# Recurrence turns: the first token-shift of the next feature tile ahead of the cumulative scan, the next weights' bf16 split in mid-turn

## The reference, cut to what matters

```
z_rw = z_rw + mu_shift * (z_prev - z_rw)
r, k, v, zw, za, zg = split(z_rw)
w_log = -softplus(-(rw_w0 + tanh(zw) @ rw_w2)) - 0.5 ; decay = exp(-exp(w_log))
state = state * w + (state @ a) b^T + v k^T          # for each token
y = state @ r  -> group norm, + bonus, * gate
```

## Time and profile before

| | |
|---|---|
| time, median of 3 | 1773.59 us (1773.27 to 1776.62) |
| profiled execution | 1781.12 us |
| its span, first to last instruction | 1779.3 us |
| mean granted TensorE clock | 0.985 of full speed |
| PE busy | 1659.7 us, 93% |
| DVE, ACT, POOL busy | 756.4 us (43%), 562.1 us (32%), 452.4 us (25%) |
| the recurrence's turns | about 155 to 484 us of the span |

### The profile page before, as it was taken

How to read it: one execution, slowest core, us unless ns; L and a number is a source line. 1 busy time by engine, 2 the same in 40 slices (tenths; PEclk the granted TensorE clock), 3 DMA queues, 4 the chain that set the end, 5 groups by cost and what they waited for, 6 DMA issues and landing times. The chain is left out here.

```text
span 1779.3 us, 35511 instructions
## 1 busy us (share of the span) xinstructions
PE 1659.7 (93%) x15497; PEld 864.6 (49%) x15690; DVE 756.4 (43%) x1040; ACT 562.1 (32%) x882; POOL 452.4 (25%) x236
## 2 busy tenths in 40 slices
PE   4999888898899999799999899999999999999997
PEld 2454655566644555444444344444444444444443
DVE  5596545555433555411311288332314233232328
ACT  5323444444323555321212156330202121121200
POOL 1221311222201112022522213461505232332220
PEclk9999999999999999999999999999999999999999
DMA  9851001000111200221210211331212020212002
GB/s 356 259 190 31 15 4 30 12 9 22 47 29 48 60 1 1 104 74 35 62 44 24 95 48 36 95 95 48 64 42 83 19 76 24 71 35 83 1 0 95
DMA packets 105775, 109.72 MB, mean 62 GB/s; under 512 B 2592, under 2 KB 82610, under 8 KB 105394
## 3 DMA queue, kind: packets, MB, share of 16 engines
q1 hardware_dynamic: 105648, 107.82, 18.7%
HBM read 101.52 MB, written 4.19 MB: 59 GB/s over the span
## 5 line engine op out<-in xcount | busy, mean ns | idle before, releaser
L218 PE MATMUL tokens_ps<-a_hi,z 128*128 128x512 bf16 x941 | 246.0, 381 | 4.0 <-ACT ff_r L2426 3.0
L674 PE MATMUL ff_ps<-ff_hi,c_lo 128*128 128x512 bf16 x503 | 190.6, 379 | 0.6
L674 PE MATMUL ff_ps<-ff_hi,c_hi 128*128 128x512 bf16 x501 | 189.9, 379 | 1.4 <-DVE z L2530 0.9
L674 PE MATMUL ff_ps<-ff_lo,c_hi 128*128 128x512 bf16 x501 | 189.9, 379 | 0.6
L2530 DVE TENSOR_TENSOR z<-ff_ps,z 128x512 f32<-128x512 f32 x128 | 88.3, 690 | 205.1 <-PE ff_ps L674 204.4
L2426 ACT ACTIVATE ff_r<-tokens_ps,cols 128x1024 f32<-128x1024 f32 x32 | 35.6, 1113 | 436.2 <-PE tokens_ps L218 427.0
L2353 POOL TENSOR_TENSOR z<-z 128x1024 bf16<-128x1024 f32 x28 | 62.2, 2220 | 351.6 <-ACT z L2349 351.6
L218 PEld LDWEIGHTS tokens_ps<-a_hi,z 128*128 128x128 bf16 x960 | 94.1, 98 | 116.6 <-issue 4.0
L218 PE MATMUL tokens_ps<-a_lo,z 128*128 128x512 bf16 x469 | 140.9, 380 | 0.6
L2518 DVE TENSOR_TENSOR ff_r<-ff_r 128x1024 f32<-128x1024 f32 x32 | 41.1, 1285 | 226.2 <-ACT ff_r L2426 226.2
L195 POOL TENSOR_TENSOR mg_wlo<-mg_stage,mg_whi 128x1024 bf16<-128x1024 f32 x21 | 45.6, 2176 | 158.1 <-ACT mg_whi L191 158.1
(11 more groups left out here) (374 smaller groups left out, 3071.2 us busy)
## 6 DMA issues: line engine op xcount, KB each, us to landing
ff_st<-w_ff SPq DMA_DIRECT2D x8, 2048.0 KB, 7.7
z<-w_ff SPq DMA_DIRECT2D x30, 512.0 KB, 4.0
ada_w<-w_ada SPq DMA_DIRECT2D x6, 2048.0 KB, 8.6
z<-w_in SPq DMA_DIRECT2D x18, 512.0 KB, 4.4
z<-w_ada SPq DMA_DIRECT2D x8, 1024.0 KB, 13.4
mg_stage<-w_in SPq DMA_DIRECT2D x16, 512.0 KB, 4.1
zs_stage<-w_in SPq DMA_DIRECT2D x8, 512.0 KB, 6.8
ada_w<-w_ada SPq DMA_DIRECT2D x4, 1024.0 KB, 13.5
```

The source lines that it names most:

```text
L218: last = pe.matmul(out[:, h * HALF:(h + 1) * HALF], w[:, kt, :], a[:, slot, h * HALF:(h + 1) * HALF], start=(x == 0 and y == 0), stop=(x = ...
L674: last = pe.matmul(out, a[:, slot, at], w[:, x, n], start=(x == 0 and y == 0), stop=(x == k - 1 and y == 2))
```

## The change

ACT's `dense_high(t + 2)` stood near the end of the turn, behind `high(lll)` and ahead of `answers(l)`. It now stands behind the copy of the transposed keys (`natural(t, "kn", ...)`) and ahead of `correction(t, 3)`. DVE's `shift(2 * n)` stood behind `cumulate(n)`, `gained(lll)` and `added(lll)`. From turn 1 on it now stands ahead of the three; in turn 0 it stays, as `shift(2)`. No wait inside a step is changed, nor any instruction's data.

```diff
@@ ScalarE, turn(t)
                 decays(n)
                 natural(t, "kn", flat(kn[:]), BB[:])
+                dense_high(t + 2)
                 if t == TURNS - 1:
                     value_weight(PAIRS + 1)
                 correction(t, 3)
...
                 high(lll)
-                dense_high(t + 2)
                 if t == TURNS - 2:
                     value_weight(2)
                 answers(l)
@@ VectorE, turn(t)
                 inverse(t, 1)
                 state(l, 2)
+                if t:
+                    shift(2 * n)
                 cumulate(n)
                 gained(lll)
                 added(lll)
-                shift(2 * n)
+                if t == 0:
+                    shift(2)
                 state(l, 3)
                 inverse(t, 2)
```

## The result

The changed kernel takes 1765.3 us (median of 12 runs, 1759.9 to 1769.1), the kernel before 1775.0 us (12 runs, 1771.7 to 1779.8; the three runs of its table are among them). The ratio is 0.9943 with a 95% interval of 0.9931 to 0.9955: 10.1 us less, between 8.0 and 12.2. It is faster by more than 0.2%. The forecast was 13.1 less, so 1760.5 us. What was measured lies outside the forecast's own range (1757.5 to 1763) and inside the range of 8 in 10 (1756.5 to 1767).

What follows compares the result with a forecast made beforehand. PE was taken to bound the kernel, through its waits in the recurrence's turns. Waits for the shift 7.4, for the split 2.9 and clock 2.8 sum to 13.1 us: 1773.6 - 13.1 = 1760.5 us, 8-in-10 range 1756.5 to 1767.

Steps and rivals of the forecast that it cites:

- The term of 7.4: Mid-turn in turns 1 to 4, projection waits for DVE's token saving shrink: 1.13 + 1.13 + 2.65 + 2.47 = 7.4 us.
- The 0.17 taken back in turns 3 and 4: The `chain` matmul would wait for DVE's state step, giving back 0.17 us in each of these turns.
- What the shift pays: The scan starts about 0.85 us later in four turns; taken as 0 because PE steps cover it, otherwise 3.4 us.
- Two falls of three gone for good: Behind mid-turn waits of turns 2 to 4, PE's half-clock falls cost 4.1 us; 2.8 us of that was counted as gained.
- the rival of the clock falling elsewhere: PE's clock falls as often as before, at other places; 10.3 us gained, time 1763.3 us; chance 17%.
- the 1.4 us of the prediction: Cost of a clock fall from the mid-turn resume to `correction(t, 3)`: 1.39 us in turn 2, 1.40 in turn 4.
- The split: ACT's `dense_high` copy moved to mid-turn removes PE's waits where turns 1 to 3 begin: 2.9 us in sum.
- the rival of the instructions: PE's instructions arrive no faster, so unexplained gaps early in turns grow; 7.6 us left, time 1766.0 us; chance 12%.
- Turns 3 to 5: Split gains nothing there: POOL takes `low(t - 3)` first, so waits where turns 4 to 6 begin stay, longest 1.5 us.
- The cover of ACT: The split's 1.05 us copy hides in ACT's mid-turn gap; taken as 0, bounds 0 and 6.3 us.
- The slower rival: On ACT ahead of `correction(t, 3)`, split and later exponentials delay the copy of `X`; time 1780.4 us; chance 4%.
- a wait put down to the wrong engine: Mid-turn wait is only named after DVE, the inverse's own chain ends as late; time 1770.7 us; chance 7%.

Runs made afterwards that it cites:

- The low part first: Changed kernel with POOL making the low part of the next weights ahead of the low part of turn t - 3's output: ratios 0.9924 and, repeated, 0.9926.
- the projection between: Six projection matmuls moved between the small ones early in a turn, on the kernel with POOL's low part of the weights first: 1759.4 us, ratio 0.9924.

## Why the prediction was right or wrong

- **The shift: right as a mechanism, a little too large.** The waits for line 1348 went as worked out, 0.46 left in turn 1 against 0.44 (both read at the second matmul). The term of 7.4 rests on waits that were each read one matmul too long. From the full profiles (1.34, 1.11, 2.42, 2.42) and the 0.23 that is left it is 7.1. The 0.17 taken back in turns 3 and 4 came of the same missing record: with 0.06 from release to PE in place of 0.28, the state step would have let `chain` go at 343.11, ahead of 343.16, and nothing of the 0.17 was seen. Turns 1 to 4 agree, 7 us shorter with the shift alone.
- **What the shift pays: right.** The later scan cost PE nothing: no wait for an exponential, the keys' copy or POOL's front appeared.
- **The clock: the step that failed, in its size.** "Two falls of three gone for good" took the three falls of one execution for what is usual. Five profiles with the mid-turn waits have 6 falls behind them, 1.2 in each. These are gone, none in nine profiles, so that part of the mechanism was right. But where turns 4 to 6 begin, falls went from 5 in five profiles to 9 in the six that keep those waits, which is the rival of the clock falling elsewhere. Together 2.2 falls in each profile became 1.5, and 0.7 fall at the 1.4 us of the prediction is about 1.0 us, an estimate from small counts, not 2.8. The runs allow the same size. Within one kernel and group, a run is 0.7 us longer for each 0.001 of mean clock that it has less (86 runs), and the mean clock is 0.0018 higher with the shift alone (0.9860 against 0.9842), which gives 1.3 us, an estimate too. With 7.1 from the waits that is 8.1 to 8.4, inside the 7.3 to 12.2 that the shift alone measured. Why the clock falls behind a wait in one execution and not in another stays open.
- **The split: right in what it removes, wrong in what that is worth.** The waits where turns 1 to 3 begin are gone, and PE reached line 1801 at 225.98, 0.25 behind the end of `PQ`'s copies, as foreseen for the next limit. Yet the split alone measured between 1.4 us less and 2.3 more, not 2.9 less. Two sizes are off: those waits are worth 2.2 us or so in full profiles (1.09, 1.09 and 0.60, less 0.29 in each of the first two, which `PQ` still holds), and the gaps of PE grow by about 1.3, among them one of 0.6 to 1.2 us soon after the removed wait in turn 2. That is the rival of the instructions, limited to this part; it had put the whole kernel at 1766.0, and the median was 1765.3. That the two numbers are so near is luck in part: the rival took a quarter of the shift's share, too, and the shift alone kept at least its waits. The means of gaps rest on four and six profiles that spread by 4 us, so the 1.3 is weak; the new gap is in every one.
- **Turns 3 to 5: right.** The waits of 1.2 to 1.5 us stayed, and the reordering of POOL that removed them shows why.
- **The cover of ACT: right**, with more room than counted: the copy is not late, and 2.1 us more did not show. The slower rival is out. So is the one of a wait put down to the wrong engine: nothing took the mid-turn wait's place.
- **The base.** The sum was made in an execution whose turns were 7 us longer than those of two later ones of the same kernel. It was set against a median of three runs, 1773.6, where all 12, these three among them, gave 1775.0. The measured difference of 10.1 (8.0 to 12.2) fits 7.1 from the shift's waits, 1.0 to 1.3 estimated for the clock, and 0 to 3 from the split; the last two were not isolated in the times.

No version measured beats the changed kernel for certain. The low part first, with or without the projection between, is at 0.9924 to 0.9926 against 0.9930 and 0.9943.

## What to carry to other kernels

A wait that ends last at one place can be costed from its row, after a look whether the record of the first instruction behind it is there; what the clock did behind it can't be, until several profiles show how often it falls there: here 6 times at 20 waits. A small removed wait ahead of a run of many small instructions can be worth less than its length, as the split's was here, where PE's stream has gaps of its own. And a transfer of work to an idle engine's gap is cheap to test: do it three times and see whether anyone waits.

## What the runs showed that was not expected

- PE pauses for 0.3 to 1.9 us at places that lie whole multiples of 256 of its instructions apart. They are moved by 128 inserted instructions and not by 256, and make 5 to 12 us in total between 185 and 440 us. No other engine is waited for there.
- With the same program and waits, the granted clock fell at different places: three falls in mid-turn in one profile of the kernel before, none there in two others, and one and two in the two profiles of the split alone. Yet all falls of turns 1 to 6 stand at the end of a wait for line 1348 or 1090.
- The first turn began between 154.5 and 159.0 us (line 1498) in the twelve profiles without inserted matmuls, with no moved instruction ahead of it: a spread of one execution as large as half of the gain. PE's wait for POOL's front (line 1077) just ahead of that turn is 0.8 to 2.7 us in the same profiles.
